# Attention of a two-block kernel: both heads of a pair take each query tile together, on halves of TensorE's array

## Reference

```python
def forgetting_attention(q, k, v, f_logit):
    scale = 1.0 / float(np.sqrt(dh))
    c = jnp.cumsum(jax.nn.log_sigmoid(f_logit.astype(jnp.float32)), axis=1)
    for blk in range(s // Q_BLOCK):                       # Q_BLOCK = 128
        qs, qe = blk * Q_BLOCK, (blk + 1) * Q_BLOCK
        sc = jnp.einsum('bhqd,bhkd->bhqk', qh[:, :, qs:qe], kh[:, :, :qe]) * scale
        sc = sc + (c[:, :, qs:qe, None] - c[:, :, None, :qe])
        sc = jnp.where(causal[None, None], sc, -jnp.inf)
        pr = jax.nn.softmax(sc, axis=-1)
        outs.append(jnp.einsum('bhqk,bhkd->bhqd', pr, vh[:, :, :qe]))
```

## Time and profile before

| | us |
|---|---|
| runs: median (lowest to highest) of 3 | 3125.68 (3123.44 to 3134.28) |
| profiled execution | 3129.88 |
| its span, first to last instruction | 3128.1 |
| PE busy | 3016.4 |
| DVE busy | 2104.8 |
| ACT busy | 1422.2 |
| attention stage of layer 1, scores(0) to L2571 | 1260.9 to 1455.8 |
| attention stage of layer 2, from scores(0) | 2397.8 |

### The profile page before, as it was taken

The page is one execution under the profiler, slowest core; times in us unless marked ns, Lnnn a source line. Parts: engine busy times, 40 slices in busy tenths (PEclk is TensorE's granted clock), DMA queues, the critical chain, the costliest instruction groups (busy, mean ns, idle before and its releaser), DMA issues.

```text
span 3128.1 us, 51785 instructions
## 1 busy us (share of the span) xinstructions
PE 3016.4 (96%) x19012; PEld 2574.9 (82%) x19012; DVE 2104.8 (67%) x3101; ACT 1422.2 (45%) x2295; POOL 479.0 (15%) x392
## 2 busy tenths in 40 slices
PE   7999999999999999999999999999999999999998
PEld 4788888887799988667789987799887667799986
DVE  5665665446699745776699844899447776799635
ACT  3655555453366523334456622566323334466422
POOL 0213223075600010000200012100110000200012
PEclk9999999999999999999999999999999999999998
DMA  6112021123223222212323223233322112223321
GB/s 247 51 51 60 13 62 43 39 85 111 90 106 105 98 95 79 68 61 68 101 94 105 103 95 107 72 104 107 102 80 81 62 61 80 101 95 106 108 99 69
DMA packets 94911, 270.91 MB, mean 87 GB/s; under 512 B 35440, under 2 KB 36592, under 8 KB 93424
## 3 DMA queue, kind: packets, MB, share of 16 engines
q1 hardware_dynamic: 94016, 267.89, 25.6%
q0 software_dynamic: 320, 1.05, 0.1%
q10 hardware_dynamic: 432, 0.02, 0.0%
HBM read 263.68 MB, written 5.24 MB: 86 GB/s over the span
## 4 chain that ended last, share of the span: by engine, by line
PE 83%; DVE 7%; ACT 4%; issue 2%; SPq 2%; DMA 1%; ACTq 0%; DVEq 0%
PE bank L149 15%; PE bank L151 15%; PE bank L150 15%; PE bank L2027 8%; PE bank L2028 8%; PE bank L2029 8%; PE bank L2523 1%; PE bank L1599 1%; PE bank L2544 1%; ACT weights_hi L137 1%; SPq L665 1%; DVE weights_lo L142 1%; PE bank L1613 1%; PE bank L1665 1%; PE bank L2533 1%
## 5 line engine op out<-in xcount | busy, mean ns | idle before, releaser
L142 DVE TENSOR_TENSOR weights_lo<-weights_raw,weights_hi 128x1024 fp32r<-128x1024 f32 (+2 forms) x258 | 397.0, 1539 | 361.1 <-ACT weights_hi L137 356.9
L137 ACT ACTIVATE weights_hi<-weights_raw 128x1024 fp32r<-128x1024 f32 (+2 forms) x250 | 285.3, 1141 | 470.5 <-PE bank L151 457.5
L149 PE MATMUL bank<-x_hi,weights_hi 128*128 128x512 f32 x832 | 335.7, 403 | 9.6 <-DVE x_lo L1915 3.1
L151 PE MATMUL bank<-x_hi,weights_lo 128*128 128x512 f32 x832 | 327.9, 394 | 0.0
L150 PE MATMUL bank<-x_lo,weights_hi 128*128 128x512 f32 x832 | 327.8, 394 | 0.0
L2027 PE MATMUL bank<-sum_hi,block_hi 128*128 128x256 f32 x960 | 272.0, 283 | 4.1 <-ACT bank L2179 3.7
L150 PE MATMUL bank<-hidden_lo,weights_hi 128*128 128x512 f32 x704 | 273.9, 389 | 0.0
L149 PE MATMUL bank<-hidden_hi,weights_hi 128*128 128x512 f32 x704 | 273.9, 389 | 0.0
L151 PE MATMUL bank<-hidden_hi,weights_lo 128*128 128x512 f32 x704 | 273.9, 389 | 0.0
L2028 PE MATMUL bank<-sum_lo,block_hi 128*128 128x256 f32 x960 | 271.6, 283 | 0.0
L2029 PE MATMUL bank<-sum_hi,block_lo 128*128 128x256 f32 x960 | 270.2, 282 | 0.0
(11 more groups left out here) (454 smaller groups left out, 7510.8 us busy)
## 6 DMA issues: line engine op xcount, KB each, us to landing
raw_pair<-w_ff1in SPq DMA_DIRECT2D x42, 1024.0 KB, 4.8
raw_pair<-w_ff2in SPq DMA_DIRECT2D x42, 1024.0 KB, 4.9
weights_raw<-w_mix SPq DMA_DIRECT2D x72, 512.0 KB, 3.2
weights_raw<-w_ff1out SPq DMA_DIRECT2D x32, 704.0 KB, 4.0
weights_raw<-w_ff2out SPq DMA_DIRECT2D x32, 704.0 KB, 4.1
weights_raw<-w_tail SPq DMA_DIRECT2D x42, 512.0 KB, 3.3
mod_weights<-w_mod SPq DMA_DIRECT2D x6, 2048.0 KB, 16.1
weights_raw<-w_dn SPq DMA_DIRECT2D x24, 512.0 KB, 3.6
```

Source lines behind the costliest of these rows:

```text
L137: nc.scalar.activation(K.wh[:, slot, 0:cols], K.raw[:, slot, 0:cols], ACT.Copy).then_inc(S.wh_ready, 1)
L142: nc.vector.tensor_tensor(K.wl[:, slot, 0:cols], K.raw[:, slot, 0:cols], K.wh[:, slot, 0:cols].bitcast(F32), ALU.subtract).then_inc(S.raw_ ...
L149: nc.tensor.matmul(out, K.wh[:, slot, a:b], xh, start=start, stop=False)
L151: return nc.tensor.matmul(out, K.wl[:, slot, a:b], xh, start=False, stop=stop)
```

## The change

Steps now go by query tile and then by head: step n is pair n // 8, query tile i = n % 8 // 2, head j = n % 2. `scores(m)`, m = n // 2, issues both heads' score matmuls one behind the other, then both masks. Head 0's operands lie in partitions 0 to 63 and head 1's in 64 to 127, so the first uses the upper rows of the array and the second the lower; they write banks 3 and 4. `scores` is called in odd steps only, behind the second unit. `attend(p)` is called once a pair and alternates the two heads, whose results lie in partitions 0 to 63 and 64 to 127 of bank 7, so that one uses the left columns of the array and the other the right. A second `probs_by_key_odd` holds the odd head's turned tiles. `forget` is called one step earlier. The waits follow the new numbering.

```diff
-        def scores(n):
-            p, j, i = n // 8, n // 4 % 2, n % 4
-            if n % 8 == 0:
+        def scores(m):
+
+            p, i = m // 4, m % 4
+            if i == 0:
                 pe.wait_ge(S.evac, v1 + (6 * p - 2 if p else 1) + 3)
-            pe.wait_ge(S.neg_ready, 32 * l + n - 1 + NEG_CREDIT)
+            pe.wait_ge(S.neg_ready, 32 * l + 2 * m + NEG_CREDIT)
             w = 128 * (i + 1)
-            bank = pb[3 + n % 2]
-            nc.tensor.matmul(bank[:, 0:w], K.qts[p % 2][64 * j:64 * j + 64, 128 * i:128 * i + 128],
-                             K.kts[p % 2][64 * j:64 * j + 64, 0:w], start=True, stop=False)
-            nc.tensor.matmul(bank[:, w - 128:w], K.identr[:, :], K.futr[:, :], start=False, stop=True)\
-                .then_inc(S.sc_ready, 1)
+            for j in range(2):
+                own = slice(64 * j, 64 * j + 64)
+                nc.tensor.matmul(pb[3 + j][:, 0:w], K.qts[p % 2][own, 128 * i:128 * i + 128], K.kts[p % 2][own, 0:w],
+                                 start=True, stop=False)
+            for j in range(2):
+                nc.tensor.matmul(pb[3 + j][:, w - 128:w], K.identr[:, :], K.futr[:, :], start=False, stop=True)\
+                    .then_inc(S.sc_ready, 1)
...
-        def attend(g):
-            p, j = g // 2, g % 2
-            pe.wait_ge(S.ptc_ready, 32 * l + 4 * g + 4 + CREDIT)
-            if j == 0:
-                pe.wait_ge(S.vtok_ready, 4 * l + p + 1 + CREDIT)
-                pe.wait_ge(S.ao_ready, 4 * l + p + CREDIT)
+        def attend(p):
+            pe.wait_ge(S.ptc_ready, 32 * l + 8 * p + 8 + CREDIT)
+            pe.wait_ge(S.vtok_ready, 4 * l + p + 1 + CREDIT)
+            pe.wait_ge(S.ao_ready, 4 * l + p + CREDIT)
             for kk in range(4):
-                last = nc.tensor.matmul(pb[7][64 * j:64 * j + 64, 128 * kk:512],
-                                        K.vtok[:, kk, 64 * j:64 * j + 64], K.pt[:, kk, 128 * kk:512],
-                                        start=(kk == 0), stop=(kk == 3))
-            last.then_inc(S.at_ready, 1)
+                for j in range(2):
+                    last = nc.tensor.matmul(pb[7][64 * j:64 * j + 64, 128 * kk:512],
+                                            K.vtok[:, kk, 64 * j:64 * j + 64], K.pt[j][:, kk, 128 * kk:512],
+                                            start=(kk == 0), stop=(kk == 3))
+                    if kk == 3:
+                        last.then_inc(S.at_ready, 1)
...
             if n > 0:
                 turn(n - 1)
-            if n + 1 < STEPS:
-                scores(n + 1)
-            for u in range(*step_units(n)):
+
+            for k, u in enumerate(range(*step_units(n))):
+                if k == 2 and n % 2 == 1 and n + 1 < STEPS:
+                    scores((n + 1) // 2)
                 dense(u // 8, u % 8, u % 8 + 1)
             if n % 8 == 1:
                 values(n // 8)
-            if n % 8 in (5, 7) and n < 24:
-                forget(n // 8 + 1, n % 8 // 7)
-            if n % 4 == 0 and n > 0:
-                attend(n // 4 - 1)
+            if n % 8 in (4, 6) and n < 24:
+                forget(n // 8 + 1, n % 8 // 6)
+            if n % 8 == 0 and n > 0:
+                attend(n // 8 - 1)
```

More of the change, by code:

```diff
@@ L230, in make_layer_memory @@
     w = at
-    K.pt = put("probs_by_key", [128, 4, 512])
+    assert w + 16384 <= TOP
+    K.pt = [put("probs_by_key", [128, 4, 512]), put("probs_by_key_odd", [128, 4, 512], F32, w + 8192)]
     K.t1 = put("t1", [128, 512], F32, w)
@@ L2514, in values @@
             last.then_inc(S.vt_ready, 1)
-        def scores(n):
-            p, j, i = n // 8, n // 4 % 2, n % 4
-            if n % 8 == 0:
+        def scores(m):
+            p, i = m // 4, m % 4
+            if i == 0:
                 pe.wait_ge(S.evac, v1 + (6 * p - 2 if p else 1) + 3)
-            pe.wait_ge(S.neg_ready, 32 * l + n - 1 + NEG_CREDIT)
+            pe.wait_ge(S.neg_ready, 32 * l + 2 * m + NEG_CREDIT)
             w = 128 * (i + 1)
-            bank = pb[3 + n % 2]
-            nc.tensor.matmul(bank[:, 0:w], K.qts[p % 2][64 * j:64 * j + 64, 128 * i:128 * i + 128],
-                             K.kts[p % 2][64 * j:64 * j + 64, 0:w], start=True, stop=False)
-            nc.tensor.matmul(bank[:, w - 128:w], K.identr[:, :], K.futr[:, :], start=False, stop=True)\
-                .then_inc(S.sc_ready, 1)
+            for j in range(2):
[5 more added lines that the diff above has]
+                    .then_inc(S.sc_ready, 1)
         def turn(n):
-            i = n % 4
+            i = n % 8 // 2
             pe.wait_ge(S.pn_ready, 32 * l + n + 1)
@@ L2572, in mix_pe @@
         dense(26, 0, 4)
-        attend(7)
+        attend(3)
         dense(26, 4, 8)
@@ L2636, in cb @@
             act.wait_ge(S.cbp_ready, 8 * l + 2 * p + j + 1 + CREDIT)
-            act.wait_ge(S.neg_ready, 32 * l + 8 * p + 4 * j - 4 + NEG_CREDIT)
+            act.wait_ge(S.neg_ready, 32 * l + 8 * p + j - 1 + NEG_CREDIT)
             nc.scalar.activation(K.cb[j][:, :], pb[2][:, :], ACT.Copy).then_inc(S.cb_ready, 1)
         def exp(n):
-            w = 128 * (n % 4 + 1)
+            w = 128 * (n % 8 // 2 + 1)
             act.wait_ge(S.neg_ready, 32 * l + n + 1 + NEG_CREDIT)
@@ L2648, in pcopy @@
         def pcopy(n):
-            i = n % 4
+            i = n % 8 // 2
             act.wait_ge(S.ptp_ready, 32 * l + n + 1 + CREDIT)
             if i == 0:
-                act.wait_ge(S.at_ready, 8 * l + n // 4 + CREDIT)
-            nc.scalar.activation(K.pt[:, 0:i + 1, 128 * i:128 * i + 128],
+                act.wait_ge(S.at_ready, 8 * l + n // 8 * 2 + CREDIT)
+            nc.scalar.activation(K.pt[n % 2][:, 0:i + 1, 128 * i:128 * i + 128],
                                  pb[5 + n % 2][:, 0:128 * (i + 1)].rearrange("p (k c) -> p k c", c=128),
@@ L2806, in logits @@
         def logits(n):
-            w = 128 * (n % 4 + 1)
-            j = n // 4 % 2
+            w = 128 * (n % 8 // 2 + 1)
+            j = n % 2
             dve.wait_ge(S.sc_ready, 32 * l + n + 1)
-            dve.wait_ge(S.cb_ready, 8 * l + n // 4 + 1)
+            dve.wait_ge(S.cb_ready, 8 * l + n // 8 * 2 + j + 1)
             dve.wait_ge(S.pe_ready, 32 * l + n - 1 + CREDIT)
```

## The result

The changed kernel takes 3079.16 us, median of four runs (3077.53 to 3081.73), beside 3127.57 for the kernel before: ratio 0.9844, 95% interval 0.9824 to 0.9864. Run again on another occasion it gave 3079.77 us, ratio 0.9837 (0.9824 to 0.9850). The forecast was 3081.5 us, range 3073 to 3104. The profiled execution went from 3129.88 to 3081.73 us, 48.2 us less where 44.2 were forecast.

What follows compares the result with a forecast made beforehand. The prediction took PE to bound the attention stage. Per layer, scores 14.2 plus attend 9.4, less 0.8 at the first turn and 0.7 of DVE stall, gives 22.1 us; 3125.68 - 44.2 = 3081.5 us, range 3073 to 3104.

Steps and rivals of the forecast that it cites:

- The bound: PE bounds layer 1's attention; PE time removed between the first turn and the sum of squares shortens the program.
- Scores: Both heads' scores of a query tile overlap on row halves, saving 3.56 us a pair, 14.2 us a layer.
- Attend: Before the sum of squares, three paired attends of 2.43 us replace seven of 2.38, saving 9.4 us a layer.
- The first turn: Ahead of the first turn, PE's idle time grows from 1.25 to 2.03 us: 0.8 us a layer given back.
- DVE's stall: PE waits on DVE, tightest in the last eight steps: 0.7 us a layer lost, between nothing and 2.
- The half-clock stretch: Behind the idle time before the first turn, granted clock 0.50 stays; the range allows 3.5 us either way.
- The sum: Over attention, 14.2 + 9.4 - 0.8 - 0.7 = 22.1 us a layer, 44.2 for two.
- The chain to the merge: PE's 1.54 us wait before the merge's convolution half ends a chain that starts at the sum of squares.
- the rival on the columns: In attend, column halves don't overlap: 2.1 us more a pair, 13.8 us less gain, 3095 us; chance 12%.
- The rule on order: In scores and attend, matmuls run strictly in program order, limiting overlap: scores save 2.5 us a pair, total 33.

## Why the prediction was right, step by step

- **The bound.** Right: PE was the bound from the first turn to the sum of squares, and the PE time taken away there came out of the total in full: the stage of layer 1 is 22.9 us shorter.
- **Scores.** 14.2 us a layer forecast, 14.0 measured by the version without them. The rows of the delta block were a good guide, though the halves here share all columns of the array. That it is overlap and not fewer entries is shown by the run on the same rows.
- **Attend.** 9.4 forecast, 9.5 measured by the same version. Column halves overlap although both read all 128 partitions; the run by head shows that order, and with it overlap, is what counts.
- **The first turn.** 0.8 us a layer given back; measured 2.00 - 1.25 = 0.75.
- **DVE's stall.** This term was mis-sized: 0.7 us a layer taken, none measured. PE has no wait over 0.1 us between the first turn and the sum of squares, in the last eight steps too. The added DVE operation shows that the slack is short all the same.
- **The half-clock stretch.** "The half-clock stretch behind it stays" was wrong for layer 2, worth 1.3 to 1.5 us. In the second run of the same kernel it was layer 1 that had none. It comes and goes from execution to execution and is no part of the change; the range allowed 3.5 us for it.
- **The sum.** 2 x 22.9 and the 1.3 of the stretch are 47.2. The other 1.0 of the 48.2 us lies outside the stages, where half-clock stretches come and go too. Behind the same 1.99 us of idle time in layer 1's merge the granted clock is 0.66 over 5 us before and 1.00 after:

```profile
1525.00:1530.00 5.00, 5.00 (x15) 3.96 (x16) 2.71 (x3) 2.28 (x3) 2.83 (x2) 0.66 0.00 2
1502.70:1507.70 5.00, 5.00 (x22) 4.15 (x23) 2.75 (x3) 2.29 (x3) 2.84 (x2) 1.00 0.02 5
```

- **Luck.** The gain was underrated by 4.0 us: 1.7 by the two stages, 1.4 of it the stall, 1.3 by the stretch and 1.0 outside the stages; the last two differ from execution to execution. The forecast took its 44.2 from a median of 3125.68; beside the changed kernel the kernel before took 3127.57, and this alone brought the measured time 1.9 us nearer to the forecast.
- **The chain to the merge.** "The chain to that point starts at the sum of squares" was wrong. It starts with slab 27's end, through an ACT split. The forecast did not rest on it, since the attend behind the sum of squares takes the same before and after (2.3 us). The price of the rival on the columns did: of the 2.1 us more of that attend it counted 0.6, and nothing of it would have been hidden.
- **The rule on order.** By the Trainium skill (TensorE: Matmul & The Clock Gate, "The mechanism") matmuls start and end strictly in program order. The trace disagrees: with attend by head, a record of the odd head starts while three earlier ones of the even head have not. One sentence of the same section has it that a weight load overlaps running matmuls only where the row group differs; another allows it for a load into the background weight buffer too. By the first each attend of a pair would have paid some 0.4 us more, by the prediction's estimate. The trace disagrees with the first and goes with the second. The pair takes 2.31 us for 2.10 of streaming, and the even head's second load, on the same rows, starts 0.06 us into its first record, whose successor comes at 1312.71:

```profile
1312.29 0.14 PEld L2547 LDWEIGHTS bank<-probs_by_key,values_by_token 128*64 128x64 f32 x1
```

## What to carry to other kernels

Where TensorE is the bound and a float32 matmul uses half its rows or half its columns, look for a partner on the other half and issue the two next to each other: the second was all but free here, on row halves and on column halves. Keep full-array instructions out from between them. Read the price of a wait from what stands behind it: PE's idle time ahead of the first turn and ahead of the merge each came from the order of one engine's program, and each went when one operation of that program stood earlier.

## What the runs showed that was not expected

- PE takes a waiting record for the other half of the array out of order. With the paired scores the second head's first record starts beside the first head's first, ahead of its second. With attend it started 1.56 us behind the first with four matmuls in front, 0.91 with three, at once with two: each time when three records, or one whole matmul, stood between. Across a full-array mask it was not taken ahead: in the run with the masks between, the other half's first record is only the third behind the first, and waits.
- Two matmuls in a row on different halves cost one, 1.06 us for four records of 512 columns; on the same rows 1.91. With the masks it is 1.33 us, and with one mask between the scores 2.53.
- A half-clock stretch of the granted clock (0.50, 1.2 GHz) behind 2.0 us of PE idle time came in one layer and not in the other of the same execution; it costs the stage 1.5 us. Its coming doesn't follow the length of the idle time alone: in the traces of all versions, 1.25 us were followed by a stretch in both layers, 1.45 in one layer of four, 1.81 in neither of two, 2.0 in seven of twelve. Without idle time there was none, in six layers.
